# Eight norms in two halves of the tokens, interleaved with the tiles before and behind them

## The reference

```python
# first block, layer i (i = 1 here is the second layer)
x = x + 0.5 * mx[2] * swiglu(modulate(rms_norm(x, g[i, 0]), mx[0], mx[1]), gu1[i], d1[i])      # f10
x = x + mx[5] * fourier_mix(modulate(rms_norm(x, g[i, 1]), mx[3], mx[4]), w_f)                 # fo
x = x + 0.5 * mx[8] * swiglu(modulate(rms_norm(x, g[i, 2]), mx[6], mx[7]), gu2[i], d2[i])      # f11
# second block
h = layer_norm(x, ln_in_g, ln_in_b)                                                            # m0
for l in range(2):
    mix = mixer(h, l) @ w_out[l]          # conv, two attentions, gated unit; h @ w_in[l] inside
    h = layer_norm(ALPHA * h + mix, ln_mix_g[l], ln_mix_b[l])                                  # c0, c1
    f = (silu(up[..., :2816]) * up[..., 2816:]) @ w_down[l]     # up = conv3(h @ w_up[l])
    h = layer_norm(ALPHA * h + f, ln_ffn_g[l], ln_ffn_b[l])                                    # m1, end
```

## Time and profile before

| | us |
|---|---|
| median of 3 timed runs | 3704.71 (3700.85 to 3705.38) |
| the profiled execution | 3697.62 |
| its span, first to last instruction | 3695.4 |
| PE busy | 3490.1 (94%) |
| DVE busy | 1934.6 (52%) |
| ACT busy | 1252.0 (34%) |
| POOL busy | 361.2 (10%) |
| mean granted TensorE clock | 0.97 |

### The profile page before, as it was taken

The page is one execution under the profiler, slowest core; times in us unless marked ns, Lnnn a source line. Parts: engine busy times, 40 slices in busy tenths (PEclk is TensorE's granted clock), DMA queues, the critical chain, the costliest instruction groups (busy, mean ns, idle before and its releaser), DMA issues.

```text
span 3695.4 us, 40300 instructions
## 1 busy us (share of the span) xinstructions
PE 3490.1 (94%) x16978; PEld 2876.7 (78%) x16978; DVE 1934.6 (52%) x2662; ACT 1252.0 (34%) x1778; POOL 361.2 (10%) x204
## 2 busy tenths in 40 slices
PE   2999999899979999999999999989999998999998
PEld 2888888787868888788877888766788876678887
DVE  8434343566655453645344333486564648666464
ACT  4322122344433222322233222324442432445242
POOL 3311001111100000000000000320100033010001
PEclk9999999899999999999999999989999999999998
DMA  5423242010115353535222222210232212013221
GB/s 195 142 80 127 86 141 71 34 35 35 35 57 171 126 195 124 182 127 181 91 74 87 96 98 91 89 64 6 69 103 97 97 66 90 6 52 103 97 97 57
DMA packets 95797, 348.81 MB, mean 94 GB/s; under 512 B 10624, under 2 KB 11136, under 8 KB 95104
## 3 DMA queue, kind: packets, MB, share of 16 engines
q1 hardware_dynamic: 94320, 343.06, 27.6%
q10 hardware_dynamic: 1296, 3.18, 0.2%
HBM read 344.10 MB, written 2.10 MB: 94 GB/s over the span
## 4 chain that ended last, share of the span: by engine, by line
PE 84%; DVE 10%; ACT 4%; issue 1%; POOL 1%; DMA 0%; ACTq 0%; DVEq 0%; POOLq 0%
PE PS L343 83%; DVE CAC L1949 2%; ACT G L1160 1%; DVE ST L1755 1%; PE PS L419 1%; DVE WL L1517 1%; DVE X L1928 1%; DVE PTL L1738 1%; DVE G L1619 0%; ACT WH L971 0%; DVE HL L1627 0%; POOL SM L2243 0%; ACT PTH L1141 0%; DVE X L1925 0%; DVE HL L1933 0%
## 5 line engine op out<-in xcount | busy, mean ns | idle before, releaser
L343 PE MATMUL PS<-HH,WH 128*128 128x512 f32 (+1 forms) x3120 | 1193.6, 383 | 38.0 <-DVE HL L1627 16.9
L343 PE MATMUL PS<-HL,WH 128*128 128x512 f32 (+1 forms) x3120 | 1177.8, 378 | 0.0
L343 PE MATMUL PS<-HH,WL 128*128 128x512 f32 (+1 forms) x3120 | 1173.8, 376 | 0.0
L1517 DVE TENSOR_TENSOR WL<-RAW,WH 128x1024 fp32r<-128x1024 f32 x462 | 584.5, 1271 | 766.9 <-ACT WH L971 766.8
L971 ACT ACTIVATE WH<-RAW 128x1024 fp32r<-128x1024 f32 x496 | 522.4, 1057 | 1140.6 <-PE PS L343 1123.0
L343 PEld LDWEIGHTS PS<-HH,WH 128*128 128x128 f32 x3120 | 594.9, 191 | 155.4 <-DVE HL L1627 19.1
L343 PEld LDWEIGHTS PS<-HL,WH 128*128 128x128 f32 x3120 | 594.5, 191 | 109.5 <-issue 5.5
L343 PEld LDWEIGHTS PS<-HH,WL 128*128 128x128 f32 x3120 | 593.6, 190 | 108.8
L343 PE MATMUL PS<-AH,WH 128*128 128x512 f32 x1392 | 526.7, 378 | 1.7 <-DVE WL L1517 1.7
L343 PE MATMUL PS<-AL,WH 128*128 128x512 f32 x1392 | 524.1, 377 | 0.0
L343 PE MATMUL PS<-AH,WL 128*128 128x512 f32 x1392 | 522.9, 376 | 0.0
(11 more groups left out here) (275 smaller groups left out, 3253.9 us busy)
## 6 DMA issues: line engine op xcount, KB each, us to landing
RAW<-wst SPq DMA_DIRECT2D x640, 512.0 KB, 3.3
X<-xT SPq DMA_DIRECT2D x1, 2048.0 KB, 12.2
out<-X SPq DMA_DIRECT2D x8, 256.0 KB, 2.0
PTF<-cb SPq DMA_DIRECT2D x1, 1024.0 KB, 4.7
Y<-yT SPq DMA_DIRECT2D x1, 1024.0 KB, 7.6
PTF<-cb ACTq DMA_DIRECT2D x1, 1024.0 KB, 4.8
HM<-sg ACTq DMA_DIRECT2D x4, 256.0 KB, 3.7
ROPE<-rope SPq DMA_DIRECT2D x1, 512.0 KB, 4.6
```

Source lines behind the costliest of these rows:

```text
L343: return e.matmul(o, l, r, start=start, stop=stop)
L1517: e.tensor_tensor(lo, raw_block(s), f32(hi), ALU.subtract).then_inc(*did("dve_done", ("wlo", b)))
```

## The change

The norms of f10, fo, f11, m0, c0, m1, c1 and end are done in two halves of 256 tokens. The last output tile of the stage before (m = 7) is computed first for tokens 0..255 over all its weight units (`lin_last`, half 0), then for 256..511 (half 1). While half 1 runs, half 0 is added to X(7), squared, its statistics are taken and (where the tile has 11 units) its reciprocal is spread. The first `lin` of the next stage becomes `lin_first`: all k-steps for half 0, then all for half 1, with the statistics and the spread of half 1 placed behind k-steps 0 and 3 of half 0. The four weight blocks stay until half 1 has used them. VectorE and ScalarE do 16 half tiles each, half 0 first (in fo: tiles 0 to 3 half 0, 0 to 3 half 1, then 4 to 7). The sums that came in the middle or towards the end of tile 7 are now asked for within its half 0. The copy of a block within tile 7 (`stream(upto["mid", ...])`) is gone for these stages, and its block is taken by `part` inside the norm. The two loads vec2 and rope96 go from behind f11 to before it, and the output is stored in 16 pieces. The bias rewriting of X after a layer norm stays as it is, in full tiles.

```diff
+HALVED = ("f10", "fo", "f11", "m0", "c0", "m1", "c1", "end")
+def norm_order(stage):
+    runs = ((0, 4), (4, 8)) if stage == "fo" else ((0, 8),)
+    return [(k, hf) for run in runs for hf in range(2) for k in range(*run)]
...
+        def products(o, u, x, hf, start, stop):
+            s = slice(hf * 256, hf * 256 + 256)
+            (uh, ul), (hi, lo, _, rows) = u[0:2], x
+            mm(o, uh[0:rows], hi[0:rows, s], start, False)
+            mm(o, uh[0:rows], lo[0:rows, s], False, False)
+            return mm(o, ul[0:rows], hi[0:rows, s], False, stop)
+        def lin_last(tile, xs, between):
...
+            for hf in range(2):
+                bk, prior = take((*name, hf), 256)
...
+                for k, x in enumerate(xs):
+                    if (hf, k) in between:
+                        between[hf, k]()
...
+                    m = products(bk[:, 0:256], us[k], x, hf, k == 0, k == len(xs) - 1)
...
+                    if hf and us[k][3]:
+                        steps.append(("wfree", us[k][2]))
...
+        def lin_first(tiles, xs, between):
...
+            for hf in range(2):
+                for k, x in enumerate(xs):
+                    if (hf, k) in between:
+                        between[hf, k]()
+                    for i, ((name, _, _), (bk, prior)) in enumerate(zip(tiles, taken)):
...
+                        q.wait_ge(*x[2], *(() if hf else (0,)))
...
+        def begin_half(st, hf):
+            up = BEFORE[st]
+            read = [("acc read", st)] if hf else []
+            if st in NORMS:
+                stat_bank((st, hf), 7 - hf)
+                sums((st, hf), ACC, 2 * hf, 2, ("acc", up, 6), True, False, *read)
+            else:
+                stat_bank(("d", st, hf), 6)
+                sums(("d", st, hf), ACC, 2 * hf, 2, ("cadd", st, 6), True, False, *read)
+                stat_bank(("v", st, hf), 7)
+                sums(("v", st, hf), A2t, 2 * hf, 2, ("csq", st, 6), True, False)
...
+            work = {begin: lambda: begin_half(st, 0), stat: lambda: half_stat(st, 0)}
...
+            return {(0, 1): lambda: (begin_half(st, 1), half_stat(st, 1)), (0, 4): lambda: half_spread(st, 1)}
...
+                            lin_last(tile, axs, tail_work(AFTER[st], (0, 7), (1, 4), (1, 9)))
...
+                order = [(g, t) for a in (0, 2) for g in range(2) for t in (a, a + 1)] if r == 0 else [(g, t) for g in range(2) for t in range(4)]
...
+            lin_last(tile(7), fx, tail_work("f11", (0, 5), (1, 4), None))
+            half_spread("f11", 0)
...
+            lin_last(tile(7), ox, tail_work(f"c{l}", (0, 6), (1, 4), None))
+            half_spread(f"c{l}", 0)
...
+        def norm_halves(st):
+            last_square(st, 0)
+            half_root(st, 0)
+            for n, (k, hf) in enumerate(norm_order(st)):
...
+                    e.activation(hview(k, NX)[0][:, s], src, ACT.Identity, bias=bias).then_inc(*did("act_done", ("hhi", st, k, hf)))
+                if n == 1:
+                    last_square(st, 1)
+                if n == (3 if st == "fo" else 4):
+                    half_root(st, 1)
+                if n >= 3 and st != "end":
+                    part(upto[LAST[st]], 1)
...
+        def norm_halves(st, last):
...
+            last(0)
+            half_stat(st, 0)
+            for n in range(17):
+                if n < 16:
+                    tile(*order[n])
+                if n and st != "end":
+                    low(*order[n - 1])
+                if n == 1:
+                    last(1)
+                if n == (3 if st == "fo" else 4):
+                    half_stat(st, 1)
+                if n >= 4 and st != "end":
+                    part(upto[LAST[st]], 1)
```

More of the change, by code:

```diff
@@ L72, in norm @@
     def norm(st):
-        uses.extend(("n", st, k) for k in range(8))
+        if st in HALVED:
+            uses.extend(("n", st, k, hf) for k, hf in norm_order(st))
+        else:
+            uses.extend(("n", st, k) for k in range(8))
     def center(st):
@@ L427, in permute, with sums @@
             mm(bk[:, :], perm, src, True, True).then_inc(*did("pe_done", ("tile", name), *more))
-        def means(name, src, n, step, start, stop, *more, into=None):
-            if start:
-                claim(name)
-                _, prior = hold(("st", name), 512, into, ("pnread", name))
-                for p in prior:
-                    q.wait_ge(*p)
+        def sums(name, src, t0, n, step, first, last, *more):
             q.wait_ge(*step)
             for t in range(n):
-                m = mm(bank["st", name][:, t:t + 1], src[:, t * 128:(t + 1) * 128], mean, start and t == 0, stop and t == n - 1)
-            if stop:
+                m = mm(bank["st", name][:, t:t + 1], src[:, (t0 + t) * 128:(t0 + t + 1) * 128], mean, first and t == 0, last and t == n - 1)
+            if last:
                 more = ("stat", name), *more
@@ L442, in means, with stat_bank @@
                 m.then_inc(*did("pe_done", *more))
+        def stat_bank(name, into):
+            claim(name)
+            _, prior = hold(("st", name), 512, into, ("pnread", name))
+            for p in prior:
+                q.wait_ge(*p)
         def tokens(st):
@@ L447, in squares @@
         def squares(st):
-            up = BEFORE[st]
-            q.wait_ge("consts")
-            means(st, ACC, tokens(st) // 128, ("acc", up, 3 if up == "at" else 6), True, False, ("acc read", st),
-                  into=0 if up == "at" else 7)
+            up, n = BEFORE[st], tokens(st) // 128
+            q.wait_ge("consts")
+            step = "acc", up, 3 if up == "at" else 6
+            stat_bank(st, 0 if up == "at" else 7)
+            sums(st, ACC, 0, n, step, True, False, ("acc read", st))
@@ new lines, in spread_half @@
+        def spread_half(name, hf, parts):
+            bk, prior = take(("sp", name, hf), 512)
+            for p in prior:
+                q.wait_ge(*p)
+            for i, (small, step) in enumerate(parts):
+                q.wait_ge(*step)
+                for t in range(2):
+                    m = mm(bk[:, i * 256 + t * 128:i * 256 + (t + 1) * 128], sm(small, 16 + t, 1).broadcast_to([128, 128]), ident, True, True)
+                m.then_inc(*did("pe_done", ("smfree", small), *([("tile", ("sp", name, hf))] if i == len(parts) - 1 else [])))
@@ L458, in norm @@
-            spread(st, N // 128, None, ("rs", st))
+            if st not in HALVED:
+                for m in range(4, 8) if up == "at" else (7,):
+                    sums(st, G(("sq", up, m)), 0, N // 128, ("sq", up, m), False, m == 7, ("gdone", ("sq", up, m)))
+                spread(st, N // 128, None, ("rs", st))
             return [(*hview(k, N), ("h", st, k), 128) for k in range(8)]
@@ L940, in _ @@
         ffn("f10", norm("f10"))
-        modulation(len(todo))
-        upto["before fo"] = allowed()
+        assert not todo
         xs = norm("fo")
```

427 lines of the change are left out of this document (280 added, 147 removed).

## The result

| | before | after |
|---|---|---|
| median of 4 timed runs, us | 3702.78 (3699.65 to 3705.38) | 3726.11 (3724.37 to 3726.56) |
| profiled execution, its span | 3697.62, 3695.4 | 3726.29, 3724.0 |
| PE busy | 3490.1 | 3512.7 |
| DVE busy | 1934.6 | 1966.1 |

The change costs 23.3 us, ratio 1.0062 (1.0045 to 1.008): slower, where "within 0.2%" was forecast (3708.6), and 3 us outside the range. All medians in this document are of fast executions; one of the nine of before beside e17 and e18, 5863.87 us at a granted clock of 0.56, is left out. The page of the kernel after: busy time and count of each engine, the chain of waits by line, the weight loads of the main products (they answer to the earlier trace rows).

What follows compares the result with a forecast made beforehand. TensorE's products bound 83% of the span, so gains come only where it idles or runs slow. Terms -3.0 - 5.0 - 2.5 + 4.0 + 1.7 + 3.7 + 2.5 + 2.5 = +3.9 us gave 3708.6; range 3692 to 3723.

Steps and rivals of the forecast that it cites:

- The first tiles take 23.0 + 0.7: f10: time in us for the first tiles after the first product, 0.7 of it for small matmuls.
- 2.0 for the modulation blocks: f10: VectorE's four modulation blocks, no longer hidden beside half k-steps, cost 0.5 us each, 2.0 in all.
- a wait for spread 1 to 14.3: fo: VectorE's turns wait for spread 1 until 14.3 us, part of why the fifth tile waits to 22.5.
- VectorE's first turn at 9.7: c0, c1: VectorE starts its turns 9.7 us after tile 7's start, behind half 1 (end 9.0) and the spread.
- The tail: c0, c1: ScalarE's table, X rewrites and block copy, then VectorE's split, take 8.6 us after the last HH, unchanged.
- last HH at 34.65 against 33.65, 1.0 lost: m0: with turns from 8.9 us after tile 7's start, the last HH comes 1.0 us later than now.
- the three stalls: m0, m1: all three GpSimd weight splits fall into VectorE's turns, at some 2.0, 2.2 and 1.1 us.
- I take 0.7: m0: clock loss put at 0.7 us, from between 0 and 2.4, as some idle is there already.
- nothing: ScalarE's queue: moving the vec2 and rope96 loads before f11's work, where ScalarE waits for tiles, costs nothing.
- B: Rival, slower: idle moved behind first tiles and into fo lowers the clock while TensorE has full work; 3719 us, chance 0.34.
- A: Rival, faster: the overlap pays, as ScalarE's tail does not end last with an earlier last HH; 3684 us, chance 0.18.
- C: Rival: weight loads bind, 0.19 in place of 0.12 us on some 240 matmuls in seven norms; 3827 us, chance 0.02.

Runs made afterwards that it cites:

- e17: Kernel before with f10, f11 and end in halves, vec2/rope96 loads moved, ScalarE's X rewrites behind later tiles, later sums: 3688.15 us, -14.2 against before.
- e18: As e17, and GpSimd waits with its weight split until VectorE has made the copy qwide: 3682.62 us, -19.8 against before.
- e15: Changed kernel, but VectorE leaves out the subtraction of the mean in c0 and c1: +6.7 us against before (1.0012 to 1.0031).
- e13: Changed kernel with four or five matmuls of constants behind the spread of half 0 in the four layer norms: +17.5 us against before.
- e11: Changed kernel, sums of tiles 0 to 6 multiplied at k-step 1 of the last tile's half 1, not in half 0: +11.2 us against before.
- e8: Changed kernel, ScalarE's eight X rewrites behind each layer norm taken two at a time behind later tiles: +2.4 us against before.
- e5: Kernel before with only the two loads vec2 and rope96 moved, no norm in halves: -6.2 us against before (0.9983 to 1.0).
- e9: Kernel before with the two loads moved and ScalarE's X rewrites taken behind later tiles, no norm in halves: -9.8 us against before.

## Why the prediction was wrong

**f10: right wait, wrong turns.** The first product came 0.92 us behind the last tile, 1 was forecast. "The first tiles take 23.0 + 0.7" and 2.0 for the modulation blocks: 25.7, measured 27.5, at the full clock and with 1.6 us of waits for VectorE. The last tile with its small matmuls was 0.8 longer than counted as well (first product at 11.0 after its start, 10.2 forecast). 0.9 gained of 3.0. f11, without such blocks, gained 3.5 of 5.0; its first product waited too (a sum of GpSimd's, 1.12, and 1.6 for HL).

**fo: waits right, but everything 2 us late.** The fifth tile waited 5.06 us (forecast 5.2), the sixth 1.98. The step that failed is "a wait for spread 1 to 14.3": VectorE's turns went on behind it at 16.2 after the tile's start, so the fifth fc tile started at 24.5 (22.5) and the sixth at 29.4 (27.5). The eight tiles were done at 35.5, where 31.6 and 1.4 for the clock make 33.0. The clock's share was nearer: TensorE ran at 0.50 for 10.2 us from 1868.0 on but stood for 3.3 of them, and of the rest only the 4.0 us behind the sixth tile's start cost time, 2.0. +6.5 in place of +4.0.

**c0, c1: the step that failed is "VectorE's first turn at 9.7".** The forecast had the wait for the early sum in it, but priced the clock only behind the first tiles; it fell in the last tile already, behind that wait (1.88 us), and stretched half 1, the statistics and the spread, all ahead of VectorE's first turn: 2.7 late. The way from there to the last HH took 24.3 in place of 22.7, with 1.12 of wait for the second half's spread, which was no term. The first tiles were done at 43.6 in place of 36, so the idle behind them is 1.6 us and not 5; most of it had been filled by first tiles 28.9 us long. The tail was sized right (8.7 against 8.6) and started 4.3 late. +5.3 in place of +2.5; e15 shows that with less on VectorE both go, e13 that the clock alone does not bring the time back. How much of the 2.7 is the wait's doing no run separates, as e11 shortened the wait to 1.08 and did not remove it.

**m0, m1: the step that failed is "last HH at 34.65 against 33.65, 1.0 lost".** m0's +1.6 matches by luck, by two errors: +4.4 in norm, tail and clock, -2.8 by the attention's clock; the 4.4 has a gain of 0.6 by the moved loads in it. VectorE's first turn came at 10.5 after the tile's start (forecast 8.9) and the last HH at 36.6. In before it was at 34.5 and not 33.65, as tile 7 starts at 2337.40 there: a misreading of 0.8; and 8.9, the turns and the three stalls as given add up to more than 34.65, some 35.5. So 2.1 were lost and not 1.0, TensorE's wait for ScalarE behind the tail grew from 1.03 to 3.33, and TensorE ran at 0.50 for 10.2 us from 2386.8 on, where it had been 3.4 from 2386.6 on ("I take 0.7"). In m1 the first turn came at 13.4 (8.9 and 2.0 make 10.9). m1's miss of 11.6 is 4.9 of attention, 1.9 of the copy that met GpSimd's split, and some 5 of the same causes as c0: GpSimd's sum asked for in half 0, waited for and followed by the lower clock, and the tail (e11 and e8 take m1 to 6.5 and 7.8; attention apart it loses 10.4, 7.6 in e11 and 2.8 in e8). That last part is argued from these runs, not measured by itself. HL operations of 2.15 and 1.76 us beside GpSimd's splits came as forecast; so did a third stall, but of a statistics operation on two columns (L2114), 2.21 us in place of 0.16:

```profile
2358.97 2.21 DVE L2114 SCALAR_TENSOR_TENSOR SM<-SM 128x2 f32<-128x2 f32 x1
```

**The loads: "nothing" was wrong.** ScalarE issues them in 0.86 us between X(7) and the square. My text named the queue, but not who waits behind it. -6.2 us in the timed runs of e5 (3.0 by the ratio, which does not exclude nothing), 0.64 of it shown as path.

**The rivals.** B was nearest in time, 3719 against 3726, but its mechanism carries only a small part. Its sign was more time at 0.5 of the clock: the traces have 221 us of it after and 220 before. From f10 to c1, attention apart, the time that TensorE worked at 0.50 rose from 58.4 to 65.5 us, which is 3.5 us of work, where these stages lost 27.7. A had the tail as the only thing that stands against a gain: without the tail the whole change is at +2.4 (e8), against -9.8 for the same edit without halves (e9). Its first products came 5.8 us earlier in m0 (6 said) but only 2.0 in c0 (4.7 said), and did not pay. C did not come: half products start every 0.12 us where nothing is waited for (2340.51, 2340.63, 2340.75 in the last tile before m0), beside weight loads of 0.19.

**end:** -2.0 against -2.5.
